# Second layer's down projection: the remainders of its weight slabs made by GpSimd in slab order, not by VectorE

## What is computed

```python
def _swiglu(x, w_gate, w_up, w_down):
    return (jax.nn.silu(x @ w_gate) * (x @ w_up)) @ w_down

for l in range(DEPTH):                      # DEPTH = 2
    ...
    x = x + _swiglu(_rmsnorm(x, norm2_g[l]), w_ffn_gate[l], w_ffn_up[l], w_ffn_down[l])
```

## Time and profile before

| | |
|---|---|
| runs, median of 3 | 1530.49 us (1529.2 to 1532.91) |
| profiled execution | 1528.97 us, span 1526.4 us |
| mean granted TensorE clock | 0.996 of full speed |
| TensorE busy | 1488.7 us (98%) |
| VectorE busy | 1103.7 us (72%) |
| ScalarE busy | 670.4 us (44%) |
| GpSimd busy | 459.6 us (30%) |

### The profile page before, as it was taken

How to read it: one execution, slowest core, us unless ns; L and a number is a source line. 1 busy time by engine, 2 the same in 40 slices (tenths; PEclk the granted TensorE clock), 3 DMA queues, 4 the chain that set the end, 5 groups by cost and what they waited for, 6 DMA issues and landing times.

```text
span 1526.4 us, 22996 instructions
## 1 busy us (share of the span) xinstructions
PE 1488.7 (98%) x8944; PEld 1220.7 (80%) x8944; DVE 1103.7 (72%) x1469; ACT 670.4 (44%) x1145; POOL 459.6 (30%) x254
## 2 busy tenths in 40 slices
PE   8999999999999999999999999999998999999998
PEld 3555897778788878888888888878886998998997
DVE  5999888778348996558332881586878995896794
ACT  5464158852452222332332422688336552453361
POOL 0000053453444454343444423444541120110010
PEclk9999999999999999999999999999999999999999
DMA  6568720132233244453538642103322323234223
GB/s 248 164 206 296 285 79 1 51 116 83 97 113 111 71 164 155 142 163 89 177 103 291 210 142 90 42 1 84 101 91 71 111 90 132 83 97 139 71 92 116
DMA packets 73498, 189.50 MB, mean 124 GB/s; under 512 B 23600, under 2 KB 32176, under 8 KB 69296
## 3 DMA queue, kind: packets, MB, share of 16 engines
q1 hardware_dynamic: 41952, 145.18, 28.5%
q10 hardware_dynamic: 31440, 42.87, 8.7%
HBM read 155.52 MB, written 32.51 MB: 123 GB/s over the span
## 4 chain that ended last, share of the span: by engine, by line
PE 61%; DVE 21%; DVEq 6%; ACT 5%; issue 4%; POOLq 1%; DMA 1%; POOL 1%; ACTq 0%; SPq 0%
PE ps L2118 18%; PE ps L2120 18%; PE ps L2119 18%; DVE wl L1989 2%; PE ps L2267 2%; DVE wsum L1980 1%; DVE work L1372 1%; DVEq L1973 1%; PE ps L2244 1%; DVEq L1552 1%; DVEq L1981 1%; ACT prob L1147 1%; DVEq L1499 1%; ACT wh L729 1%; DVE wsum L1982 1%
## 5 line engine op out<-in xcount | busy, mean ns | idle before, releaser
L631 POOL TENSOR_TENSOR wl<-stage,wh 128x1024 fp32r<-128x1024 f32 x138 | 354.7, 2576 | 647.7 <-ACT wh L729 458.4
L729 ACT ACTIVATE wh<-stage 128x1024 fp32r<-128x1024 f32 (+2 forms) x178 | 181.0, 1023 | 219.5 <-PE ps L2120 100.3
L2118 PE MATMUL ps<-XH,wh 128*128 128x256 f32 x616 | 175.3, 285 | 7.8 <-DVE X L2010 5.0
L2120 PE MATMUL ps<-XH,wl 128*128 128x256 f32 x616 | 173.7, 282 | 0.0
L2119 PE MATMUL ps<-XLr,wh 128*128 128x256 f32 x528 | 148.7, 282 | 0.0
L2118 PE MATMUL ps<-xg2h,wh 128*128 128x512 f32 x352 | 140.2, 398 | 0.0
L2120 PE MATMUL ps<-xg2h,wl 128*128 128x512 f32 x352 | 139.2, 395 | 0.0
L2119 PE MATMUL ps<-xg2l,wh 128*128 128x512 f32 x352 | 139.2, 395 | 0.0
L2118 PEld LDWEIGHTS ps<-XH,wh 128*128 128x128 f32 x616 | 116.8, 190 | 10.6 <-DVE X L2010 5.4
L2120 PEld LDWEIGHTS ps<-XH,wl 128*128 128x128 f32 x616 | 116.8, 190 | 0.0
L2173 PE MATMUL ps<-X,slabs 128*128 128x512 f32 x224 | 101.8, 610 | 5.2 <-DMA X<-in_xT 5.2
(11 more groups left out here) (343 smaller groups left out, 3750.3 us busy)
## 6 DMA issues: line engine op xcount, KB each, us to landing
stage<-in_stream SPq DMA_DIRECT2D x178, 512.0 KB, 3.4
stage_more<-in_stream SPq DMA_DIRECT2D x34, 512.0 KB, 4.1
CPTR<-ctd_scr ACTq DMA_DIRECT2D x6, 1664.0 KB, 8.6
slabs<-in_stream SPq DMA_DIRECT2D x17, 512.0 KB, 4.9
InT<-in_scr ACTq DMA_DIRECT2D x6, 1024.0 KB, 6.7
ctd_scr<-CPp SPq DMA_DIRECT2D x4, 1152.0 KB, 7.9
ctd_scr<-CPp ACTq DMA_DIRECT2D x4, 1152.0 KB, 6.6
in_scr<-BPI SPq DMA_DIRECT2D x4, 1024.0 KB, 5.1
```

Of the source, the lines that this page charges most:

```text
L631: pool.tensor_tensor(wl[:, s, :], stage[:, (n - RAW) % STAGES, :], wh[:, s, :].bitcast(F32), ALU.subtract).then_inc(wl_ready, 1)
L729: return act.activation(o, i, ACT.Copy, **kw)
L2118: pe.matmul(o, wt[0], x[0], start=start, stop=False, skip_group_check=onto)
L2120: return pe.matmul(o, wt[1], x[0], start=False, stop=stop, skip_group_check=onto)
```

## The change

VectorE's `down_low` goes with all its calls. GpSimd's loop over all 22 rounds becomes a loop over the three parts: the rounds of the part as before, then the 8 slabs of its down projection in order, each waiting for ScalarE's rounded copy and raising `wl_ready`. The instruction itself, its operands and its semaphores stay the same; ScalarE, TensorE and SyncE are not edited.

```diff
--- before.py
+++ after.py
@@ -717,11 +717,18 @@
                 for n in range(S_UP + 3, SLABS if l + 1 < DEPTH else S_FFN):
                     remainder(SLABS * l + n)
 
-            for q in range(FB):
-                s = fast_slot(3)
-                pool.wait_ge(op_hi[3], q + 1)
-                pool.tensor_tensor(wl[:, s, 0:QT], fast_stage(pair_slab(q) + 1)[:, QT:2 * QT],
-                                   wh[:, s, 0:QT].bitcast(F32), ALU.subtract).then_inc(op_lo[3], 1)
+            for h in range(len(PARTS)):
+                for q in range(first_of(h), last_of(h) + 1):
+                    s = fast_slot(3)
+                    pool.wait_ge(op_hi[3], q + 1)
+                    pool.tensor_tensor(wl[:, s, 0:QT], fast_stage(pair_slab(q) + 1)[:, QT:2 * QT],
+                                       wh[:, s, 0:QT].bitcast(F32), ALU.subtract).then_inc(op_lo[3], 1)
+                for m in range(KT):
+                    s, w = fast_slot(m), 2 * PARTS[h][1] * P
+                    pool.wait_ge(wh_ready, plain(h, m) + 1 - RAW)
+                    pool.tensor_tensor(wl[:, s, 0:w], fast_stage(down_slab(h, m))[:, 0:w],
+                                       wh[:, s, 0:w].bitcast(F32), ALU.subtract).then_inc(wl_ready, 1)
+
 
         @block.scalar
         def _(act):
@@ -1988,11 +1995,6 @@
                 dve.wait_ge(op_hi[i], q + 1)
                 tt(wl[:, s, :], source, wh[:, s, :].bitcast(F32), SUB).then_inc(op_lo[i], 1)
 
-            def down_low(h, m):
-                s, w = fast_slot(m), 2 * PARTS[h][1] * P
-                dve.wait_ge(wh_ready, plain(h, m) + 1 - RAW)
-                tt(wl[:, s, 0:w], fast_stage(down_slab(h, m))[:, 0:w], wh[:, s, 0:w].bitcast(F32), SUB).then_inc(wl_ready, 1)
-
             def normed_t(j):
                 dve.wait_ge(xt_hi, j + 1)
                 tt(XLr[:, X5 - 1:X4, j, :], XT[:, j % 2], XH[:, X5:X4 + 1, j, :].bitcast(F32), SUB).then_inc(xt_ready, 1)
@@ -2077,20 +2079,14 @@
                     if q < last:
                         low(0, q + 1)
                         sums_last(q + 1)
-                    else:
-                        down_low(h, 0)
                     if q > first:
                         scaled(q - 1)
                     if q < last:
                         low(1, q + 1)
-                    else:
-                        down_low(h, 1)
                     if q > first and q % 2 == 0:
                         rest(q - 1)
                 other_sums(last)
-                down_low(h, 2)
                 scaled(last)
-                down_low(h, 3)
                 rest(last)
                 for m in range(KT):
                     if h + 1 < len(PARTS) and m == RING:
@@ -2101,9 +2097,7 @@
                     added = tt(X[:, m, :], X[:, m, :], scaled_down[:, m % 2, :], ADD)
                     if h + 1 == len(PARTS):
                         added.then_inc(x_ready, 1)
-                    if m < RING:
-                        down_low(h, m + RING)
-                    elif h + 1 < len(PARTS):
+                    if h + 1 < len(PARTS):
                         if m == RING:
                             low(0, last + 1)
                             sums_last(last + 1)
```

## The result

The changed kernel takes 1532.07 us (median of 22 runs, 1530.41 to 1535.42) against 1529.28 us of the kernel before (median of 22 runs beside them): ratio 1.0019, 95% interval 1.0010 to 1.0027. That is 2.8 us more, 1.5 to 4.1 by the interval. The forecast was 1534.4 us, 3.9 more than the median of 1530.49 it started from. The median of 22 runs of the kernel before lies 1.2 us under that of the first three. One of these 22 runs took 6518 us; without it their median is 1529.20.

The account below looks back on a forecast made before the run. TensorE was taken to bound the kernel, so added waits of 1.28 + 1.28 + 1.17 = 3.7 us, 3.9 with slower first matmuls, were added to 1530.5 us, giving 1534.4; range 1531.5 to 1539.0.

Parts of the forecast that it names:

- The frame: After 1252 us TensorE is the bound, waiting only 0.5 us for other engines; every added wait is added to the end.
- the fourth rival: Relief of VectorE, 96% busy in the products rounds, brings line 2047 forward; bounded by 0.5 us, 1530.0 us; chance 0.08.
- Parts one and two: At the start of each one's down projection TensorE waits 1.28 us for slab 0, queued behind GpSimd's P4 half.
- the step worked out: Part one's start: line 2054 from 1254.28, P4 half until 1256.67, slab 0 until 1259.08, stall 1.28 us.
- the three rows' sum: Expected sign: TensorE waiting for GpSimd's remainder three times, 3 to 3.5 us in sum, longest 1.3.
- Part three: At its down projection's start TensorE waits 0.70 us for slab 0, a 128x768 subtraction priced at 1.85 us.
- The hidden remainder: Line 2062, needed in slabs 0 and 1: 0.5 us to spare in parts one and two; part three loses 1.17, start included.
- Who goes first on the ports: First issued gets the port pair for the whole instruction, so line 2057, issued during slab 2, goes ahead of slab 3.
- the second rival: GpSimd keeps the ports and slab 3 goes ahead of line 2057: 5.5 us more, 1536.0 us; chance 0.33.
- The sum: Waits of 1.28 + 1.28 + 1.17 = 3.7 us, plus two first matmuls slower by 0.1: 3.9 us.
- VectorE's busy time: Expected sign: down by 27 us from the 24 removed subtractions, with GpSimd's up by 53 us.
- The third rival, the clock: TensorE's clock falls in the waits, three times 1.6 us: 8.7 us more, 1539.2 us; chance 0.04.

Follow-up runs that it names:

- e5: Kernel before, but in the products rounds slot 2's remainder (22 of 128x1024) goes from VectorE to GpSimd: 1534.43 us against 1529.66, ratio 1.0034.
- second run of the changed kernel: The changed kernel unedited, measured again beside the kernel before on one chip: 1532.49 us against 1529.36, ratio 1.0025.
- e4: Changed kernel, but GpSimd subtracts slab 0 of each part twice with a drain between: 1543.07 us against 1529.36 of the kernel before, ratio 1.0092.
- e6: Changed kernel, but each part's last round does VectorE's line 2056 scaling after the round's sums: 1543.89 us, one run, against 1529.66 of the kernel before.

## Why the prediction was right, point by point

- The frame held: after 1252 us TensorE had nearly nothing to win, and the change gave it nothing. Relief of VectorE, the fourth rival, brought nothing in the down projection, and moved into the rounds, where VectorE is busy, it costs 6.4 us of the block (e5).
- Parts one and two: 1.28 us each forecast, 1.24 and 1.20 measured. Line 2056 started 3.58 us ahead of the time at which the down projection was due (1256.44 against 1260.02), just as in the step worked out (1254.28 against 1257.86). What was forecast too much came from GpSimd's subtraction, 2.37 us instead of the 2.41 taken. In the list of waits only two of the three are put down to GpSimd, and the three rows' sum is 2.6 us, not 3 to 3.5; by the starts of the matmuls it is 3.1.
- Part three: 0.70 forecast, 0.65 measured. The price for 128x768, taken as the middle of two other sizes, 1.85 us, was 1.83.
- The hidden remainder: the margin of 0.5 us in parts one and two was 0.7 (in part one line 2064 ends at 1270.31, TensorE sees it 0.06 later and needs it 9.81 after 1261.26, at 1271.07). Part three was forecast to lose 1.17 us with the start and lost 1.19.
- Who goes first on the ports: line 2059, issued at 1264.82 while slab 2 runs, ends at 1266.96, and slab 3, issued behind it, at 1269.22; line 2064, issued while slab 3 runs, ends 1.09 us later. That is the order of the Trainium skill's "SBUF — State Buffer", section "Who interferes with whom", and the second rival, GpSimd keeping the ports, is out.
- The sum: 3.9 us forecast, and 3.8 by the starts of the matmuls: 1.24 + 1.20 + 1.19, and 0.1 each for the slower first matmul in parts one and two, as forecast. The block's 3.98 holds 0.2 us more, which is lost before the first moved instruction (from the block's start to the time at which the down projection was due it is 85.72 us against 85.51). In the block's first 5.32 us, behind the wait of 5.0 us, the granted clock is 0.50 in this execution and 0.69 in the one before; in the second run of the changed kernel 0.13 us are lost there. So that the block came within 0.1 of the forecast is in part luck. The time rose by 2.8 us, and by 3.1 in the second comparison; with the 0.8 us outside the span, which the forecast did not have, that fits. The forecast of 1534.4 lay 2.3 us above the measured median: 1.2 of it the median it started from, 0.8 the time outside the span.
- Wrong: VectorE's busy time was to fall by 27 us and fell by 15.7 (1103.7 to 1088.0), and GpSimd's was to rise by 53 and rose by 58.2. The 24 subtractions went as said. Left out was how the two engines shut each other out beside TensorE's work. VectorE's other instructions (weight sums, X additions, lines 2059 and 2064) got 12 us longer in the block. GpSimd's moved ones took 58.5 us, not the 53 taken: slab 3 took 3.4 us in parts one and two, slabs 4 to 7 there 2.5 to 2.9 and in part three 2.2 to 2.3. Nearly all of it costs TensorE nothing; what does is the P4 half ahead of each start and the hidden remainder in part three.
- The third rival, the clock, was given the right shape and not its place: waits of 1.2 us did not bring it down. Of e4's waits those of 3.74 and 3.69 us did and that of 2.60 did not; e6's of 2.40, 2.45 and 3.35 us all did. Each fall cost 1.5 to 2.8 us, where I had priced 1.6.

## What to carry to other kernels

When work moves to a slower engine, the cover of its steady state says little: look at the first item behind a change of phase, what already stands ahead of it in the new engine's queue, and when the consumer starts. Here the same 24 instructions cost 4.0 us in one order and 0.55 in another. VectorE and GpSimd did not work as two engines here when both read two operands from SBUF, so a busy VectorE was not relieved by handing over an instruction that then held the ports twice as long (e5), and every chain that alternates between the two should be laid out with the other's longest instruction in it. And before a small difference in time is explained, set it beside the span and one stretch of the trace: here 0.8 us lay outside both.

## What was not expected of the hardware

- TensorE's clock after a wait does not follow from the length of that wait alone: 2.60 us in part three of e4 left it at 1.00, 2.40 us in part one of e6, 9.7 us after another wait of 0.67 us, brought it to 0.53 in the mean of the next 3.3 us. What else decides stays open.
- One more GpSimd instruction of 2.4 us in a round made a VectorE addition of 0.69 us last 2.73 in more than half of 11 rounds.
